# Residual kept in DRAM during an expert loop: 20 slots for weight tiles instead of 18, and another order of the experts

## What is computed

```python
logits = (t @ w_router + b_router).astype(jnp.float32)
top_val, top_idx = lax.top_k(logits, TOP_K)
probs = jax.nn.softmax(top_val, axis=-1)
...
def expert_block(args):
    xb, e = args
    gu = xb @ w_gate_up[e] + b_gate_up[e]
    x_glu = jnp.minimum(gu[:, 0::2], SWIGLU_LIMIT)
    x_lin = jnp.clip(gu[:, 1::2], -SWIGLU_LIMIT, SWIGLU_LIMIT)
    act = x_glu * jax.nn.sigmoid(SWIGLU_ALPHA * x_glu) * (x_lin + 1)
    return act @ w_down[e] + b_down[e]
...
x = x + mod_lat[5] * moe_ffn(h_lat, ...)
return rmsnorm(x, final_norm_g)
```

## Time and profile before

| | us |
|---|---|
| median of 3 executions | 3447.2 |
| lowest, highest | 3446.58, 3449.01 |
| the profiled execution, its own time | 3429.11 |
| its span, first to last instruction | 3427.0 |
| PE busy | 3021.9 (88%) |
| DVE busy | 985.5 (29%) |
| ACT busy | 651.3 (19%) |
| POOL busy | 190.4 (6%) |
| data moved by DMA | 580.92 MB |

### The profile page before, as it was taken

The page is one execution under the profiler, slowest core; times in us unless marked ns, Lnnn a source line. Parts: engine busy times, 40 slices in busy tenths (PEclk is TensorE's granted clock), DMA queues, the critical chain, the costliest instruction groups (busy, mean ns, idle before and its releaser), DMA issues.

```text
span 3427.0 us, 45853 instructions
## 1 busy us (share of the span) xinstructions
PE 3021.9 (88%) x19729; PEld 1556.8 (45%) x19729; DVE 985.5 (29%) x1996; ACT 651.3 (19%) x1345; POOL 190.4 (6%) x180
## 2 busy tenths in 40 slices
PE   6898879999788999899889958599999998999883
PEld 3554334444344666666656645343333333333332
DVE  2244231000312221455544553421122211212114
ACT  1133000000002333344444431111011101010100
POOL 0000000000000000111111111010000000000002
PEclk9999889999898999999999977699999999999986
DMA  4135112212110013211111100278899999999995
GB/s 151 48 146 202 68 37 85 74 49 98 56 34 26 33 44 114 109 43 44 44 44 44 43 13 2 100 282 326 328 384 383 388 396 397 391 376 398 398 362 220
DMA packets 116621, 580.92 MB, mean 170 GB/s; under 512 B 10212, under 2 KB 21508, under 8 KB 69828
## 3 DMA queue, kind: packets, MB, share of 16 engines
q1 hardware_dynamic: 92464, 531.94, 39.2%
q10 hardware_dynamic: 17652, 24.25, 1.9%
q0 software_dynamic: 6304, 21.80, 1.8%
HBM read 549.48 MB, written 28.47 MB: 169 GB/s over the span
## 4 chain that ended last, share of the span: by engine, by line
PE 75%; DMA 12%; DVE 9%; ACT 2%; issue 1%; ACTq 0%; SPq 0%; POOL 0%; DVEq 0%; POOLq 0%
PE product_banks L833 38%; PE product_banks L1192 13%; DMA space<-in_wgu 10%; PE product_banks L1214 7%; PE score_banks L1095 3%; PE out_bank L960 1%; PE out_bank L880 1%; PE score_banks L897 1%; PE turn_bank L870 1%; PE out_bank L919 1%; DVE sq L1558 1%; PE score_banks L941 1%; DVE space L1779 1%; PE score_banks L938 1%; PE product_banks L820 1%
## 5 line engine op out<-in xcount | busy, mean ns | idle before, releaser
L833 PE MATMUL product_banks<-space 128*128 128x512 f32 (+2 forms) x4016 | 1437.2, 510 | 35.9 <-DVE space L1779 13.4
L833 PEld LDWEIGHTS product_banks<-space 128*128 128x128 f32 x4016 | 710.1, 195 | 646.5 <-issue 584.1
L1192 PE MATMUL product_banks<-space 128*32 128x512 f32 x5440 | 659.0, 619 | 73.9 <-DMA space<-in_wgu 73.8
L1192 PEld LDWEIGHTS product_banks<-space 128*32 128x32 f32 x5440 | 158.4, 111 | 450.2 <-issue 297.6
L1214 PE MATMUL product_banks<-space,rstd 128*32 128x256 f32 x5440 | 321.9, 390 | 1.1 <-ACT rstd L1497 0.6
L1912 DVE TENSOR_TENSOR sq<-product_banks,cst 128x512 f32<-128x512 f32 x85 | 58.8, 692 | 774.9 <-PE product_banks L1192 774.9
L1305 ACT ACTIVATE space<-product_banks 128x512 f32<-128x512 f32 (+1 forms) x234 | 114.3, 525 | 854.9 <-PE product_banks L833 837.1
L1214 PEld LDWEIGHTS product_banks<-space,rstd 128*32 128x32 f32 x5440 | 181.4, 114 | 170.6 <-issue 71.9
L746 POOL TENSOR_TENSOR space<-space 128x512 f32<-128x512 f32 x112 | 132.4, 1194 | 1026.8 <-ACT space L1438 930.0
L1095 PE MATMUL score_banks<-space 128*128 128x64 f32 x896 | 132.9, 301 | 28.0 <-issue 21.1
L1095 PEld LDWEIGHTS score_banks<-space 128*128 128x128 f32 x896 | 129.5, 222 | 36.9 <-issue 32.5
(11 more groups left out here) (287 smaller groups left out, 2281.7 us busy)
## 6 DMA issues: line engine op xcount, KB each, us to landing
space<-in_wgu SPq DMA_DIRECT2D x256, 1024.0 KB, 18.8
space<-in_wdn SPq DMA_DIRECT2D x128, 1024.0 KB, 22.7
space<-in_wt SPq DMA_DIRECT2D x104, 1024.0 KB, 5.1
y_rows<-zeros ACTq DMA_DIRECT2D x2, 6400.0 KB, 29.4
y_rows<-zeros ACTq DMA_DIRECT2D x84, 128.0 KB
space<-in_wt SPq DMA_DIRECT2D x13, 512.0 KB, 4.4
space<-in_wt SPq DMA_DIRECT2D x4, 768.0 KB, 4.3
x<-in_xT SPq DMA_DIRECT2D x1, 2048.0 KB, 16.0
```

The lines of the kernel that those rows point to most:

```text
L833: ins = nc.tensor.matmul(bank[0:rows, at:at + cols], lhsT, rhs, start=(i == 0), stop=(i == len(mm) - 1))
L1192: ins = nc.tensor.matmul(bank[ROWS * g:ROWS * g + ROWS, :], xT_[:, k, :], w[:, 512 * g:512 * g + 512], start=(k == 0), stop=(k == DC - 1))
```

## The change

1. Two slots more: `NS = 20`. Slots 18 and 19 are the two halves of the buffer x.
2. A DRAM tensor `x_kept` of 2 MB. SP stores x there when it is complete (`s_res` at 2), ahead of the stores of the h rows; tile 18, the first that lands in x, waits for this store. After the last down product SP loads x back, and DVE's `residual(0)` waits for that.
3. `BLOCKS_AT` is written out: 2, 3, 2, 5, 1, 3, 2, 4, 2, 2, 4, 2, 2, 3, 2, 5, 2, 3, 2, 3, 2, 3, 3, 2, 3, 2, 6, 1, 4, 2, 2. The multiset is that of `RANKS`. `RANK_AT` and all the tables made from it follow.
4. The two waits on `s_hst` and `s_xtp` are tied to the tile numbers 13 and 15 by name (`H3_SLOT`, `HR_SLOT`), the same numbers as before.

```diff
-NS = 18
-SLOT0 = SPACE - NS * SLOT
+NS_SPACE = 18
+NS = NS_SPACE + 2
+SLOT0 = SPACE - NS_SPACE * SLOT
+H3_SLOT = (SPACE - RING * SLOT - SLOT0) // SLOT
+HR_SLOT = H3_SLOT + 2
...
-BLOCKS_AT = [RANKS[r] for r in RANK_AT]
+BLOCKS_AT = [2, 3, 2, 5, 1, 3, 2, 4, 2, 2, 4, 2, 2, 3, 2, 5, 2, 3, 2, 3, 2, 3, 3, 2, 3, 2, 6, 1, 4, 2, 2]
...
+        slots += [x_cols[:, SLOT * i:SLOT * i + SLOT] for i in range(2)]
...
+                sp.wait_ge(s_res, 2)
+                sp.dma_start(xkept, x).then_inc(s_xkept, 16)
...
-                        if g == NS - 5:
+                        if g == H3_SLOT:
                             sp.wait_ge(s_hst, 16 * TT)
-                        if g == NS - 3:
+                        if g == HR_SLOT:
                             sp.wait_ge(s_xtp, 1)
+                        if g == NS_SPACE:
+                            sp.wait_ge(s_xkept, 16)
...
+                sp.wait_ge(s_dn, n_more + N_FIXED_BLOCKS)
+                sp.dma_start(x, xkept).then_inc(s_xback, 16)
...
                 dve.wait_ge(s_tTc, i + 1)
+                if i == 0:
+                    dve.wait_ge(s_xback, 16)
```

## The result

| | before | after |
|---|---|---|
| median, us | 3444.3 (6 executions, 3438.4 to 3449.0) | 3422.4 (6 executions, 3415.3 to 3431.3) |
| ratio, 95% interval | | 0.9943, 0.9930 to 0.9956 |
| the profiled execution, us | 3429.1 | 3431.3 |
| its span, us | 3427.0 | 3429.3 |

The change takes 22 us off, and 3422 was measured where 3424 was forecast.

What follows compares the result with a forecast made beforehand. The prediction took the DMA weight stream as the bound, standing still for 69 us. Its terms, -28 (standstills), +2 (other traffic) and +3 (loading x), gave -23 us: 3447.2 to 3424 us, range 3409 to 3442.

Steps and rivals of the forecast that it cites:

- The pauses: Weight stream in the expert loop: standstills of 10, 10 and 21 us at the experts of 5, 5 and 6 blocks.
- Term one: Expert loop: weight-stream standstill falls from 69 to 41 us, -28 us, nearly all of it from the two extra slots.
- the law: Weight slots: a slot frees only in its expert's last block; with 20, standstills are 10.0 (5 blocks), 20.8 (6), none (4).
- The last block near 3298: End of the expert loop: by the tiles the last block starts at 3297.5 us, against 3326.97 before.
- other traffic +2: Gathers and row stores in the loop: those no longer hidden in standstills cost the tiles 2 us.
- PE has some 5 us in hand: End of the expert loop: PE could reach the last block at 3293, the tiles allow 3297.5.
- Storing x: Before the loop, on SP's queue: the 2 MB store fits where DMA is idle, cost 0.
- Loading x: After the last down product: 2 MB take room on the DMA engines before store and gathers, +3 us (0 to 10).
- No pause left: Rival, expert loop: slots freed earlier let the weight stream run through, 3383 us; chance 0.04.
- The order gives the gain back: Rival, expert loop: PE lags at the large experts, standstills add up to 68 us, 3451 us; chance 0.07.
- Pitch above 2.887: Rival, weight stream: time per tile grows beside stores and gathers, making the kernel slower, 3474 us at 2.96; chance 0.08.
- The load on the end's path: Rival, kernel's end: loading x back costs +10 to +13 us instead of +3, 3431 to 3434 us; chance 0.07.

Runs made afterwards that it cites:

- x_again: The kernel after, unaltered, run and traced a second time: median 3421.7 us, ratio 0.9938.
- x_keep: The kernel before plus the store and load of x and their waits, still 18 slots and the old order: 3447.9 us, ratio 1.0011.
- b_again: The kernel before, unaltered, run and traced a second time: median 3444.6 us, ratio 1.0016 to its own twin.
- x_noload: The kernel after without the load of x back and DVE's wait for it, so the output leaves out the residual: 3419.3 us.
- x_order: The kernel before with the new order of experts alone, 18 slots, x left in place: 3439.1 us, ratio 0.9994.
- y_spread: The kernel after with each fixed block's output rows stored by four DMAs of 32 rows by 256 columns, not one: 3369.6 us, ratio 0.9794.

## Why the prediction was right

The number was, and in part by luck. Its largest term was twice too large as it was argued; an effect that the first trace did not show made up for half of that, and 4 to 6 us of the rest have no cause that the traces show.

*The pauses* (41 us forecast). 10.5, 11.8 and 20.8 in after, 10.9, 11.0 and 19.9 in x_again: 43 and 42. The places were right too.

*Term one, -28, "nearly all of it from the slots".* Measured between traces with the usual entry it is 1122.8 to 1102.0 or 1099.0, **-21 to -24**, of which some 7 are the late entry taken up, which the prediction did not know of: the first trace showed the short one. The pauses and all that goes with them brought 1116.3 to 1102.0 or 1099.0, **-14 to -17**, half of the forecast. And the slots alone bring 1122.8 to 1111.6, -11, not the -25 of "with the old order, 20 slots would give 24, 10, 10: about 44". The parts fit together so: the order is worth -7 by the entry in both cases, and by the law +3 with 18 slots (72 for 69) and -3 with 20 (41 for 44); that is -4 (measured 1121.2 - 1122.8 = -2) and -10 (measured -10 and -13).

*The last block near 3298.* It started 1102.0 and 1099.0 behind the first issue, where the forecast has 3297.5 - 2210.65 = 1086.9. The 15.1 and 12.1 us are made of these, for after and x_again:

| | after | x_again |
|---|---|---|
| the three pauses, over 41 | 2.1 | 0.8 |
| 204 tiles at 2.871 and 2.863 in place of 2.824 | 9.6 | 8.0 |
| the last block is set by PE, not the tiles | 4.4 | 4.4 |
| first 43 tiles | -0.8 | -0.9 |
| sum | 15.3 | 12.3 |

So the **pitch** is the term that was mis-sized: "other traffic +2" measured 8 to 10. The 9.6 of after have three parts. The pitch of 2.824 was itself a mean: in before's trace the tiles come at 2.839 from place 18 to 28, where experts of 3 and 2 blocks take turns (3255.32 - 2914.60 = 340.7 us for 120 tiles), and at 2.749 in the last 24 tiles; at 2.839 the 204 tiles take 3.1 us more. Behind the two experts of 4 blocks at places 7 and 10 come 3.3 more (1.7 in x_again): the forecast pause "below zero" for these, from one mean pitch, overlooked that twelve engines run dry before the last four. And 3.4 fall between places 19 and 26, where no expert has more than 3 blocks; what makes the tiles late there is open. *"PE has some 5 us in hand"* was wrong: it is 4 us late. From the landing at 3248.42 the tiles would have allowed 3248.42 + 24 x 2.824 + 4.4 = 3320.6, and PE came at 3325.05, after 4, 2 and 2 blocks in a row. (The 4.4 is the prediction's; in before the last block started 5.7 behind its last up tile, so up to 1.3 of the lateness may be this step.)

*What made up for it.* The late entry, -7, above. With the tail's +5 to +6 the traces give -16 to -18 in all, inside the interval of the ratio (-15 to -24) but not its middle; the other 4 to 6 us of the median's -22 can't be given to any part of the change, since the loop begins anywhere in 13 us.

*Storing x, 0.* It landed in 6.3 us, x_keep's loop is that of b_again (1122.9 and 1122.8), and it begins no later behind x. Right.

*Loading x, +3.* 5.0 us in the traces of the store's landing, 2 to 4 in the medians of x_keep and x_noload. The mechanism was right: the cost is room, not the wait. The estimate of 6.8 us by the page "DMA: Bandwidth & Descriptors" (section Anatomy of one DMA) is near the store's 6.3 and below the load's 7.9; the page fits it to DMAs issued from GpSimd, and these are issued by SP. That by the page the load would cost 1 and the time be 3422 was refuted, though 3422 was measured: the load was over before the first gather, but the gathers wait for a store that had to share with it.

*The rivals.* No pause left: three are there. The order gives the gain back: with 18 slots it neither gives nor takes (x_order, -5 within the noise of 0.16%), with 20 it adds. Pitch above 2.887: 2.87, near but under; 2.88 was the prediction's bound for being wrong; the stretch from place 19 to 26 is at it (241.9 / 84 = 2.88), and one (104.3 / 36 = 2.90) is above. The load on the end's path: not by DVE's wait.

## What to carry to other kernels

Where a stream of weights waits for slots, count a pause as the time until the first release less the tiles that fit ahead, and then compare stream and engine stretch by stretch, the first one too: in this kernel the order that opens with the engine's largest piece paid for 9 us of lateness at the entry in full, the one that opens with small pieces not at all. Ask of a small store beside a saturated stream on how many DMA engines it is laid, and not only how many bytes it has: a DMA share that stands at a simple fraction when the stream runs out (here 0.26), or while the store runs alone (0.25), is the sign. A term that rests on one stretch of one trace wants a second trace, or a bound for what that stretch usually takes.

## What the hardware showed unasked

11 MB of output rows (84 stores of 128 KB), 3% of what the loop moves beside 390 MB of weights, cost some 50 us more in the four-piece form than in that of y_spread. And one trace of the eleven had a loop entry of 11.3 us where the others have 18.8, with the same instructions.
